# Chunked scans whose outputs leave the array as tokens by channels, and the order of the steps around them

## The reference

```
def step(S, inp):
    r_t, w_t, k_t, v_t, kk_t, a_t = inp
    sa = -jnp.einsum('dbhij,dbhj->dbhi', S, kk_t)
    S = (S * w_t[..., None, :]
         + sa[..., :, None] * (kk_t * a_t)[..., None, :]
         + v_t[..., :, None] * k_t[..., None, :])
    return S, jnp.einsum('dbhij,dbhj->dbhi', S, r_t)
...
_, out = lax.scan(step, S0, xs)
out = jnp.moveaxis(out, 0, 2)
return out[0] + jnp.flip(out[1], axis=1)
...
mean = jnp.mean(o, axis=-1, keepdims=True)
var = jnp.mean(jnp.square(o - mean), axis=-1, keepdims=True)
o = ((o - mean) * lax.rsqrt(var + RWKV_GN_EPS)).reshape(B, T, RWKV_WIDTH)
o = (o * gn_w.astype(jnp.float32) + gn_b.astype(jnp.float32)).astype(r.dtype)
...
return (o + bonus) * g
```

## Time and profile before

| what | us |
|---|---|
| median of 3 runs | 2369.81 (2368.15 to 2372.09) |
| the profiled execution, its own time | 2367.51 |
| its span in the profile | 2365.7 |
| PE busy | 2317.4 (98%) |
| DVE busy | 1510.5 (64%) |
| ACT busy | 1104.3 (47%) |
| POOL busy | 131.4 (6%) |
| scans, from the last gate product to the first product of `p_ya` | 1303.4 to 1450.8 |

### The profile page before, as it was taken

How to read it: one execution, slowest core, us unless ns; L and a number is a source line. 1 busy time by engine, 2 the same in 40 slices (tenths; PEclk the granted TensorE clock), 3 DMA queues, 4 the chain that set the end, 5 groups by cost and what they waited for, 6 DMA issues and landing times.

```text
span 2365.7 us, 32698 instructions
## 1 busy us (share of the span) xinstructions
PE 2317.4 (98%) x12307; PEld 1899.5 (80%) x12307; DVE 1510.5 (64%) x2003; ACT 1104.3 (47%) x1456; POOL 131.4 (6%) x209
## 2 busy tenths in 40 slices
PE   8999999999999999999999999999999999999998
PEld 6888888888887878778877777887888888888886
DVE  5666754666756666997963556666667664466665
ACT  5454443444445665555565323444544443444443
POOL 1000000000000002221011210000000000000000
PEclk9999999999999999999999999999999999999999
DMA  7666666666665756678677212765766666666654
GB/s 246 196 194 195 189 196 194 188 198 192 194 195 178 232 170 189 198 218 288 198 225 206 85 42 99 233 234 164 220 194 190 196 192 195 194 190 195 195 194 145
DMA packets 229697, 451.51 MB, mean 191 GB/s; under 512 B 23420, under 2 KB 25744, under 8 KB 228176
## 3 DMA queue, kind: packets, MB, share of 16 engines
q1 hardware_dynamic: 207872, 399.82, 55.1%
q0 software_dynamic: 11600, 45.31, 5.8%
q10 hardware_dynamic: 10112, 4.83, 0.8%
HBM read 427.35 MB, written 22.54 MB: 190 GB/s over the span
## 4 chain that ended last, share of the span: by engine, by line
PE 90%; DVE 4%; DMA 2%; ACT 2%; issue 1%; POOL 0%; ACTq 0%; DVEq 0%; SPq 0%; POOLq 0%
PE ps L1616 27%; PE ps L1618 27%; PE ps L1617 27%; DVE wlo L999 1%; DMA raw<-in_w_in 1%; PE ps L1976 1%; PE ps L2017 1%; PE ps L2002 1%; PE ps L2018 1%; PE ps L1977 1%; PE ps L1992 1%; DMA xin<-dif_dram 1%; PE ps L2033 1%; PE ps L2037 0%; DVE h L1088 0%
## 5 line engine op out<-in xcount | busy, mean ns | idle before, releaser
L999 DVE TENSOR_TENSOR wlo<-raw,whi 128x1024 fp32r<-128x1024 f32 (+1 forms) x760 | 929.8, 1228 | 691.2 <-ACT whi L516 686.4
L516 ACT ACTIVATE whi<-raw 128x1024 fp32r<-128x1024 f32 (+1 forms) x760 | 800.8, 1058 | 944.1 <-PE ps L1618 898.4
L1616 PE MATMUL ps<-whi,uhi 128*128 128x512 f32 (+1 forms) x2272 | 897.0, 395 | 8.2 <-DVE ulo L1038 4.1
L1618 PE MATMUL ps<-whi,ulo 128*128 128x512 f32 (+1 forms) x2272 | 885.8, 390 | 0.0
L1617 PE MATMUL ps<-wlo,uhi 128*128 128x512 f32 (+1 forms) x2272 | 885.4, 390 | 0.0
L1616 PEld LDWEIGHTS ps<-whi,uhi 128*128 128x128 f32 x2272 | 427.7, 188 | 106.2 <-issue 11.5
L1618 PEld LDWEIGHTS ps<-whi,ulo 128*128 128x128 f32 x2272 | 427.5, 188 | 89.0
L1617 PEld LDWEIGHTS ps<-wlo,uhi 128*128 128x128 f32 x2272 | 428.2, 188 | 84.6
L1616 PE MATMUL ps<-whi,hthi 128*128 128x512 f32 x704 | 274.0, 389 | 0.0
L1618 PE MATMUL ps<-whi,htlo 128*128 128x512 f32 x704 | 274.0, 389 | 0.0
L1617 PE MATMUL ps<-wlo,hthi 128*128 128x512 f32 x704 | 274.0, 389 | 0.0
(11 more groups left out here) (303 smaller groups left out, 1454.6 us busy)
## 6 DMA issues: line engine op xcount, KB each, us to landing
raw<-in_ffn_w_gu SPq DMA_DIRECT2D x352, 512.0 KB, 4.4
raw<-in_ffn_w_down SPq DMA_DIRECT2D x176, 512.0 KB, 4.4
raw<-in_w_in SPq DMA_DIRECT2D x160, 512.0 KB, 3.9
raw<-in_w_out SPq DMA_DIRECT2D x32, 512.0 KB, 4.0
raw<-in_w_branch_a SPq DMA_DIRECT2D x16, 512.0 KB, 4.2
raw<-in_w_branch_b SPq DMA_DIRECT2D x16, 512.0 KB, 3.9
gate_dram<-gst_g POOLq DMA_DIRECT2D x8, 512.0 KB, 5.4
gbuf<-gate_dram POOLq DMA_DIRECT2D x8, 512.0 KB, 4.8
```

Of the source, the lines that this page charges most:

```text
L516: nc.scalar.activation(whi[:, s, :, 0:p.width], raw[:, s, :, 0:p.width], ACT.Copy).then_inc(hi_ready, 1)
L999: V.tensor_tensor(wlo[:, s, :, 0:p.width], raw[:, s, :, 0:p.width], whi[:, s, :, 0:p.width].bitcast(F32), ALU.subtract).then_inc(lo_ready, 1)
L1616: mm(o, at, w_, start=(j == 0 and k == 0), stop=False)
L1618: return mm(o, bt, w_, start=False, stop=(j == p.slots - 1 and k == SB - 1))
```

## The change

The scans' outputs are now tokens by channels. In `recur` both products of a chunk have `gh` as the stationary operand and `sv` as the moving one; the state goes to partitions 64 to 127 and the outputs of both heads to partitions 0 to 63, both in bank 7. ACT takes the outputs out of bank 7 (`outputs`, new, two copies for a scan, the backward direction into a tile of its own, `ob`), in place of DVE's `to_oc`. `values_t` is two full transposes in place of four products, and its values go to partitions 0 to 63 of `sv` with two copies on ACT. `alpha_beta` writes banks 2 and 3, `w_products` bank 1 and `values_t` bank 0.

With tokens on the partitions, the sums over a head's channels are made by DVE's reductions along the row (`gn_center`, `gn_variance`), so the two products of ones are gone; root and reciprocal run over 128x4 values. The normalized pair is turned back to channels by tokens by two transposes (`gn_turn`), behind the first chunk of odd rounds, and `ya_out` applies scale, bias, bonus and gate in two instructions. On DVE `ends` stands directly behind `masked_gh`, ahead of the steps of the norm (`norm_behind`) and of the `ahead` splits. On ACT `values(m + 1)` stands behind the first copy of the state, `gn_square` behind the second. For the first scan, `alpha_beta(0)` waits for the pair of banks 2 and 3 alone; the wait for banks 0 and 1 stands behind it, and `values_t(0)` stands ahead of `w_products(0)`.

```diff
-                nc.scalar.activation(sv[C:P, m % 2, :, :], ps[C:P, 2, :].rearrange("p (c v) -> p c v", c=NC_),
-                                     ACT.Copy).then_inc(vt_ready, 1)
+                for e in range(2):
+                    last = nc.scalar.activation(sv[0:C, m % 2, e::2, :],
+                                                ps[C * e:C * (e + 1), 0, 0:2 * P].rearrange("p (k v) -> p k v", v=P), ACT.Copy)
+                last.then_inc(vt_ready, 1)
...
+            def outputs(m):
...
+                b, d = m // 2, m % 2
+                act.wait_ge(o_mm, m + 1)
+                if d and b >= 2:
+                    act.wait_ge(gn_cent, b - 1)
+                chunks = ps[0:C, 7, :].rearrange("p (c v) -> p c v", c=NC_)
+                dst = (ob[:, b % 2, :] if d else oc[:, b, :]).rearrange("p (k v) -> p k v", v=P)
+                for e in range(2):
+                    last = nc.scalar.activation(dst[C * e:C * (e + 1), :, :],
+                                                chunks[:, ::-1, :][:, e::2, :] if d else chunks[:, e::2, :], ACT.Copy)
+                last.then_inc(o_ready, 1)
...
                     minus_w(m + 1)
-                    values(m + 1)
                 for c in range(NC_ - 1):
                     act.wait_ge(s_mm, 3 * m + c + 1)
-                    nc.scalar.activation(sv[0:C, m % 2, c + 1, :], ps[0:C, 2, 0:2 * C], ACT.Copy).then_inc(s_ready, 1)
+                    nc.scalar.activation(sv[C:P, m % 2, c + 1, :], ps[C:P, 7, c * P:(c + 1) * P], ACT.Copy).then_inc(s_ready, 1)
...
+                    if c == 0 and m + 1 < NM:
+                        values(m + 1)
+                    if c == 1 and m % 2 == 0 and m:
+                        gn_square(m // 2 - 1)
+                outputs(m)
                 if m < RING:
...
-                if m % 2:
-                    if b >= 0:
-                        gn_deviation(b)
-                else:
-                    if b >= 1:
-                        ya_high(b - 1)
-                    if b >= 0:
-                        gn_square(b)
+                if m % 2 == 0 and m:
+                    gn_deviation(m // 2 - 1)
+                if m % 2 and m >= 3:
+                    ya_high((m - 3) // 2)
...
             def gn_center(b):
-                dve.wait_ge(gn_mean, b + 1)
-                V.scalar_tensor_tensor(out=oc[:, b, :], in0=ps[:, 6, 0:T], scalar=-1.0 / C, in1=oc[:, b, :],
-                                       op0=ALU.mult, op1=ALU.add).then_inc(gn_cent, 1)
+
+                dve.wait_ge(o_ready, 2 * b + 2)
+                y = oc[:, b, :]
+                link(V.tensor_tensor(y, y, ob[:, b % 2, :], ALU.add))
+                link(V.tensor_reduce(GN_MEAN, by_head(y), AX.X, ALU.add))
+                link(V.tensor_scalar(GN_MEAN, GN_MEAN, 1.0 / C, None, ALU.mult))
+                V.tensor_tensor(by_head(y), by_head(y), GN_MEAN.unsqueeze(2).broadcast_to((P, 4, C)),
+                                ALU.subtract).then_inc(gn_cent, 1)
+
+            def gn_variance(b):
+                dve.wait_ge(gn_sq, b + 1)
+                V.tensor_reduce(GN_VAR, by_head(osq[:, b % 2, :]), AX.X, ALU.add).then_inc(gn_ms, 1)
 
             def gn_scale(b):
...
+                y = by_head(oc[:, b, :])
+                link(V.reciprocal(GN_DEV, GN_DEV))
+                V.tensor_tensor(y, y, GN_DEV.unsqueeze(2).broadcast_to((P, 4, C)), ALU.mult).then_inc(gn_scaled, 1)
...
+            def ya_out(b):
+                dve.wait_ge(gn_t, b + 1)
...
-                link(V.reciprocal(rs[:, b % 2, :], rs[:, b % 2, :]))
-                link(V.scalar_tensor_tensor(out=y, in0=y, scalar=vec[:, R_GNW + b:R_GNW + b + 1],
-                                            in1=rs[:, b % 2, :], op0=ALU.mult, op1=ALU.mult))
-                link(V.scalar_tensor_tensor(out=y, in0=y, scalar=vec[:, R_GNB + b:R_GNB + b + 1], in1=bo[:, b % 4, :],
-                                            op0=ALU.add, op1=ALU.add))
-                V.tensor_tensor(y, y, gg[:, b % 4, :], ALU.mult).then_inc(ya_y, 1)
+                link(V.scalar_tensor_tensor(out=y, in0=ps[:, 6, 0:T], scalar=vec[:, R_GNW + b:R_GNW + b + 1],
+                                            in1=bo[:, b % 4, :], op0=ALU.mult, op1=ALU.add))
+                V.scalar_tensor_tensor(out=y, in0=y, scalar=vec[:, R_GNB + b:R_GNB + b + 1], in1=gg[:, b % 4, :],
+                                       op0=ALU.add, op1=ALU.mult).then_inc(ya_y, 1)
...
-                b = m // 2 - 1
                 if m % 2 == 0:
-                    if b >= 1:
-                        gn_scale(b - 1)
-                    if b >= 0:
-                        gn_center(b)
+                    if m:
+                        gn_variance(m // 2 - 1)
+                    if m >= 4:
+                        ya_low(m // 2 - 2)
+                elif m >= 3:
+                    ya_out((m - 3) // 2)
+
+            def norm_behind(m):
+
+                if m % 2:
+                    gn_center(m // 2)
+                elif m:
+                    gn_scale(m // 2 - 1)
...
-            def to_oc(m):
-                b = m // 2
-                dve.wait_ge(o_mm, m + 1)
-                src = ps[:, 7, 0:T]
-                if m % 2:
-                    V.tensor_tensor(oc[:, b, :], oc[:, b, :], src[:, ::-1], ALU.add).then_inc(o_ready, 1)
-                else:
-                    V.tensor_copy(oc[:, b, :], src).then_inc(o_ready, 1)
...
+            ends(2)
             dve.wait_ge(st_out[0], 16 * 7)
             dve.wait_ge(st_out[1], 16 * 7)
             for m in range(NM):
                 if m + 2 < NM:
-                    ends(m + 2)
                     masked_ab(m + 2)
                 else:
                     norm_between(m)
-                if m % 2 and m >= 5:
-                    ya_low(m // 2 - 2)
-                to_oc(m)
-                dve.wait_ge(o_ready, m + 1)
                 if m + 1 < NM:
...
                     masked_gh(m + 1)
+                if m + 3 < NM:
+                    ends(m + 3)
+                norm_behind(m)
                 if m < RING:
...
-            gn_center(NPAIR - 1)
-            gn_scale(NPAIR - 2)
             ya_low(NPAIR - 2)
+            gn_variance(NPAIR - 1)
+            gn_scale(NPAIR - 1)
...
-                for c in range(NC_):
-                    last = mm(ps[C:P, 2, c * P:(c + 1) * P], vt[:, c * C:(c + 1) * C], ident, start=True, stop=True)
+                for k in range(NT):
+                    last = nc.tensor.transpose(ps[:, 0, k * P:(k + 1) * P], vt[:, k * P:(k + 1) * P], ident)
...
+                def half(rows_, cols, h):
+                    return mm(ps[rows_, 7, c * P + h * C:c * P + (h + 1) * C], gh[:, m % 2, NC_ * h + c, cols],
+                              sv[:, m % 2, c, h * C:(h + 1) * C], start=True, stop=True)
...
                 if c < NC_ - 1:
-                    for h in range(2):
-                        last = mm(ps[0:C, 2, h * C:(h + 1) * C], gh[:, m % 2, NC_ * h + c, C:2 * C],
-                                  sv[:, m % 2, c, h * C:(h + 1) * C], start=True, stop=True)
-                    last.then_inc(s_mm, 1)
-                for h in range(2):
-                    last = mm(ps[C * h:C * (h + 1), 7, c * C:(c + 1) * C], sv[:, m % 2, c, h * C:(h + 1) * C],
-                              gh[:, m % 2, NC_ * h + c, 0:C], start=True, stop=True)
+                    half(slice(C, P), slice(C, 2 * C), 0)
+                    half(slice(C, P), slice(C, 2 * C), 1).then_inc(s_mm, 1)
+                half(slice(0, C), slice(0, C), 0)
+                last = half(slice(0, C), slice(0, C), 1)
...
+            def gn_turn(b):
+                pe.wait_ge(gn_scaled, b + 1)
                 if b:
-                    pe.wait_ge(gn_sqrt, b)
-                mm(ps[:, 6, 0:T], headsum, oc[:, b, :], start=True, stop=True).then_inc(gn_mean, 1)
-
-            def gn_variances(b):
-                pe.wait_ge(gn_sq, b + 1)
-                mm(ps[:, 6, T:2 * T], headsum, osq[:, b % 2, :], start=True, stop=True).then_inc(gn_var, 1)
-
-            gates_out(0)
+                    pe.wait_ge(ya_y, b)
+                for k in range(NT):
+                    last = nc.tensor.transpose(ps[:, 6, k * P:(k + 1) * P], oc[:, b, k * P:(k + 1) * P], ident)
+                last.then_inc(gn_t, 1)
...
+            gates_out(1)
             for c in range(NC_):
                 alpha_beta(0, c)
-            gates_out(1)
+            gates_out(0)
+            values_t(0)
             w_products(0)
-            values_t(0)
             for c in range(NC_):
                 alpha_beta(1, c)
...
-                    if c == 0 and m >= 2:
-                        gn_means(m // 2 - 1) if m % 2 == 0 else gn_variances(m // 2 - 1)
+                    if c == 0 and m >= 3 and m % 2:
+                        gn_turn((m - 3) // 2)
...
-            gn_means(NPAIR - 1)
             fill = filler(in_steps(p_ya, product(p_ya, lambda u, k: yahi[:, k, :], lambda u, k: yalo[:, k, :],
```

(6 more changed lines are left out.)

72 lines of the change are left out of this document (38 added, 34 removed).

## The result

| what | before | after |
|---|---|---|
| median | 2368.98 us (4 runs, 2365.45 to 2372.09) | 2352.26 us (4 runs, 2350.48 to 2352.94) |
| ratio | | 0.9932, interval 0.9919 to 0.9944 |
| profiled execution, its span | 2367.51, 2365.7 | 2352.94, 2351.1 |
| last gate product starts | 1303.39 | 1304.99 |
| w products of round 0 start (W0) | 1314.52 | 1318.03 |

What follows compares the result with a forecast made beforehand. PE, busy for 98% of the span, was taken as the bound. Rounds -11.6, start +0.2, end -1.8 and clock +3.2 gave -10.0 us, 2357.5 for the profiled execution; 2.3 more for a median gave 2359.8 us, range 2353.5 to 2365.

Steps and rivals of the forecast that it cites:

- The start of the recurrence: Each scan round: first recurrence starts 1.40 us (1.35 to 1.5) after the round's w products start (W).
- the last chunk: End of each scan: both output products write the same 64 array columns, adding 0.11 us (0 to 0.2).
- the new wait ahead of the turn: Odd rounds: PE waits 0.46 us (0.2 to 0.8) for DVE's scaling of the norm before the turn's transposes.
- The term that failed: Recurrences of the other three chunks: 0.49 us kept, 0.06 less if the column halves overlap, 0.12 more if not.
- rival (B): Scan rounds: array halves don't overlap and the turn waits longer; with the clock's fall, 2368 us; chance 0.12.
- -11.6: Rounds 0 to 13 of the scans: eight at 7.70 and six at 8.46 us, 11.6 us faster (8 to 15).
- The clock's term: Start of the scans: a 4.0 us PE wait brings 6.8 us at half clock, costing 3.2 us.
- The rest of the start: Up to the first gh products: still waiting for the `vb` load, +0.2 us (-0.3 to +0.5) without the clock.
- The end: Behind round 13: shorter last steps and no wait for `to_oc`, -1.8 us (-1 to -2.5).
- (A): Rival at the start of the scans: the clock holds, total -13.2 us, 2356.6 us; chance 0.30.
- the short side of the rounds: Rounds 0 to 13: the smallest gain in their range, 8 us instead of 11.6, used for the high end.
- (D): Rival in the scan rounds: ACT or DVE take PE's place, 12 us eat the gain, 2370 us; chance 0.05.

Runs made afterwards that it cites:

- Experiment 4: Changed kernel with the decay diagonals behind the steps of the norm on DVE again, ahead of the next masks: 2368.75 us.
- experiment 9: Kernel before the change with the norm's reciprocal on 4 of 256 columns only, the rest left out: 2363.59 us.
- experiment 1: Changed kernel with the state products of chunks 1 and 2 written to the array columns that the output products use: 2357.58 us.
- experiment 7: Changed kernel with six products whose result nobody reads ahead of `values_t(0)`, in PE's wait for the `vb` load: 2353.11 us.
- experiment 5: Changed kernel with the turned norm behind the second chunk of odd rounds instead of the first: 2352.82 us, repeated 2348.69 us.
- experiment 8: Repeats: changed kernel 2351.17 us, with early `vb` load and later turn 2344.79; the latter with unread products in last-round waits 2345.01, plus last chunk's outputs in both halves 2342.59.

## Why the prediction was wrong

**The direction and most mechanisms were right.** The start of the recurrence (W + 1.39, forecast 1.40), the beta products brought forward, the last chunk (+0.12, forecast 0.11), the wait for the mask gone, the new wait ahead of the turn (0.38, forecast 0.46) and its slot (0.36, forecast 0.30), ACT's copies of 0.38 each and nothing late behind them in rounds 0 to 13: all as written. Experiment 4 shows how much the order on DVE is worth, experiment 9 the reciprocal.

**The term that failed is the recurrence.** "They took 0.49; I keep 0.49, with 0.06 less if the halves overlap and 0.12 more if they don't." The overlap was likely, not a side case: in the kernel before, the values (columns 64 to 127) already ran beside the state's products (columns 0 to 63), and the forecast cites that only against rival (B). And its size is 0.10: the 0.49 had six records in the fuller half and the change leaves four, which is 0.12 less by the rule and 0.10 less by the rows. Three times 0.10 in a round is 0.3, over 14 rounds 4.2 us, which is the difference between -11.6 and -15.8. With it the plain round is 7.70 - 0.30 = 7.40 (measured 7.38). The count of products was read, and not where each writes. Only the 0.12 was right: that is what chunks 1 and 2 of experiment 1 took more than 0.49.

**The clock's term was twice too large.** The fall came at the place and for the reason named, but lasted 3.4 us and not 6.8, and cost 1.6 (experiment 7) where 3.2 were written. The rest of the start was right: 13.04 - 1.6 = 11.4 against 11.13 before, +0.3 where +0.2 was forecast. One observed fall was taken as the size of the next; at this very place two executions of one kernel had 3.4 and 6.8 us (experiment 5).

**The end.** Forecast -1.8, measured -2.3: -1.6 up to `p_ya` and -0.7 behind it. There the first four slots took 11.97 us in the kernel before, 11.57 with the short reciprocal of experiment 9, and 11.27 in the changed one: 0.4 is the last norm's reciprocal, which the forecast did not have as a wait of the fourth slot, and 0.3 the turn in place of a product of ones. The chain of ACT and DVE held without a gap in front of the fourth slot. One wait of PE was overlooked: in round 14, without beta products, the copies of the values (0.77 us) make the second state copy late, the row with 0.64 above; the next recurrence comes 1.10 us behind the one before it, where the others come 0.81. And the shorter recurrence gains next to nothing in rounds 14 and 15: from one recurrence to the next pass 0.81 us there in both kernels, and PE waits 0.35 for ACT where it waited 0.24.

**The range.** Its low end took (A) and 2.9 us of overlap; the sum is 2356.6 - 2.9 = 2353.7, the text has 2353.5. The high end, 2365, does not come out of its parts exactly either: the short side of the rounds alone gives 2363.4, with half of (B) 2367.5. Nor does (D): 12 us on top of 2359.8 are 2371.8, where 2370 is written. With 0.10 instead of 0.06 for the 42 recurrences of rounds 0 to 13 the overlap is 4.2, which puts the low end at 2352.4, 0.1 above the measured time; and that end also takes the clock to hold at the start, which it did not.

**From 2359.8 to 2352.26.** In the two traces the kernel gained 14.6 and not 10.0 us: 4.2 more in the rounds, 1.5 less lost at the start, 0.5 more at the end, and 1.6 lost ahead of the scans, where nothing was changed and the clock near 1255 makes most of it. The other 3.0 us are no term of the sum. The forecast added 2.3 for where the profiled execution lay under its median, and that of the changed kernel lay 0.7 above its own. The medians of such a kernel move by 1 to 4 us between sets of four or five runs (experiments 5 and 8), so this part is luck either way. With every term of the traces right, the same sum would have given 2355.2.

**Still open:** what decides how long a fall lasts at one place, and how many of them the executions without a profile have.

## What to carry to other kernels

Count a group of small products by the columns of the array that each writes, not by their number: the group takes as long as its fuller column half, here 0.058 us for each record of 128x64. State and outputs in different halves were worth 0.10 us a recurrence, 4.2 us in 14 rounds, as long as other work on PE followed; where only the wait for the next state followed, nothing. A wait of PE costs more than its length if the clock falls behind it; at the start, work of no use in the wait kept the clock, and moving the load ahead of the wait gave both. Where executions of one kernel differ by some us, judge an edit of 1 to 3 us by the distances between marks in the trace (round to round), and repeat the measurement before believing a median.

## What the runs showed that I had not expected

- Float32 products of 128x64 over all 128 rows, with outputs in different column halves, start 13 ns apart; with the same columns each starts 0.058 us behind the one before it.
- Stretches at half clock lasted 3.4, 6.8, 10.2 or 13.7 us by the granted clock. They cost half their length or less, 1.6 us for 3.4 at the start and 4.2 for 10.2 near 1255, where part of the stretch fell into PE's wait. In one and the same kernel the stretch near 1255 was 0 and 10.2 us long, behind waits of 2.73 and 3.83 us.
- Such stretches also began where PE only had waits of 0.35 to 1.27 us (the last two rounds), in ten of thirteen executions, and in none of two where products filled these waits. The waits of 0.38 in odd rounds, with transposes behind them, had none behind them in the five executions that have them.
